# A four-layer float32 transformer on one core: the on-chip buffers get new start addresses

## The reference

```python
def first_block(x, ...):                       # two layers
    for l in range(DEPTH):
        n = rms_norm(h, attn_norm[l])
        h = h + (hybrid_mixer(n, ...) if l % 2 == 0 else diff_mixer(n, ...))
        h = h + conv_glu_ffn(rms_norm(h, ffn_norm[l]), ffn_w_up[l], ffn_conv_w[l], ffn_conv_b[l], ffn_w_down[l])
    return rms_norm(h, final_norm)

def conv_glu_ffn(n, w_up, conv_w, conv_b, w_down):      # D_FF = 2816
    gate, up = jnp.split(n @ w_up, 2, axis=-1)
    ...
    return (jax.nn.silu(conv) * up) @ w_down

def second_block(x, ...):                      # two layers
    h = layer_norm(x, ln_in_g, ln_in_b)
    for l in range(DEPTH):
        h = layer_norm(DN_ALPHA * h + token_mixers(h, ...), ln1_g[l], ln1_b[l])
        h = layer_norm(DN_ALPHA * h + conv_ffn(h, ...), ln2_g[l], ln2_b[l])
    return h
```

## Time and profile before

| | us |
|---|---|
| median of 3 runs | 2945.43 (2944.07 to 2948.2) |
| span of the profiled execution | 2941.9 |
| what lies around the span, against the median | 3.5 |
| busy: PE, PE weight loads | 2746.1, 2003.8 |
| busy: DVE, ACT, POOL | 1738.8, 1095.4, 1045.3 |

### The profile page before, as it was taken

How to read it: one execution, slowest core, us unless ns; L and a number is a source line. 1 busy time by engine, 2 the same in 40 slices (tenths; PEclk the granted TensorE clock), 3 DMA queues, 4 the chain that set the end, 5 groups by cost and what they waited for, 6 DMA issues and landing times.

```text
span 2941.9 us, 34757 instructions
## 1 busy us (share of the span) xinstructions
PE 2746.1 (93%) x11434; PEld 2003.8 (68%) x11434; DVE 1738.8 (59%) x2256; ACT 1095.4 (37%) x1682; POOL 1045.3 (36%) x385
## 2 busy tenths in 40 slices
PE   6999999999998999999698988999989998899997
PEld 5654788887764678888375455778757644577875
DVE  4645774576386576377559336827634944583672
ACT  2344322223144343222442545323345345532333
POOL 3210344443321244444144123544424411254442
PEclk9998999999998899999799999999999998999999
DMA  3210223232211123222111011222311110122231
GB/s 134 65 50 22 65 92 106 87 101 85 79 51 36 43 87 105 87 94 99 39 54 54 29 37 64 95 90 93 102 61 55 51 43 22 64 93 96 90 97 67
DMA packets 56070, 212.17 MB, mean 72 GB/s; under 512 B 6192, under 2 KB 6448, under 8 KB 55856
## 3 DMA queue, kind: packets, MB, share of 16 engines
q1 hardware_dynamic: 55120, 209.60, 21.5%
q10 hardware_dynamic: 864, 1.44, 0.2%
HBM read 208.92 MB, written 2.10 MB: 72 GB/s over the span
## 4 chain that ended last, share of the span: by engine, by line
PE 78%; DVE 9%; issue 5%; ACT 5%; POOL 2%; DVEq 1%; DMA 0%; ACTq 0%; POOLq 0%
PE bank_G L457 22%; PE bank_G L459 21%; PE bank_G L458 21%; PE bank_S L1086 4%; PE bank_O L1096 2%; PE bank_X L1106 2%; DVE mx L1978 2%; PE bank_S L504 1%; POOL wlo L404 1%; PE bank_X L1651 1%; DVE scores_t L1629 1%; POOL decayed L1771 1%; DVE probs L1159 1%; PE bank_O L1722 1%; PE bank_X L786 1%
## 5 line engine op out<-in xcount | busy, mean ns | idle before, releaser
L404 POOL TENSOR_TENSOR wlo<-raw,whi 128x1024 fp32r<-128x1024 f32 (+1 forms) x363 | 1002.3, 2762 | 1762.3 <-ACT whi L430 1762.2
L457 PE MATMUL bank_G<-n_hi,whi 128*128 128x512 f32 x2392 | 980.3, 410 | 62.3 <-DVE n_lo L561 29.7
L459 PE MATMUL bank_G<-n_hi,wlo 128*128 128x512 f32 x2392 | 948.9, 397 | 0.0
L458 PE MATMUL bank_G<-n_lo,whi 128*128 128x512 f32 x2392 | 947.8, 396 | 0.0
L457 PEld LDWEIGHTS bank_G<-n_hi,whi 128*128 128x128 f32 x2392 | 457.9, 191 | 208.7 <-issue 65.8
L430 ACT ACTIVATE whi<-raw 128x1024 fp32r<-128x1024 f32 (+1 forms) x363 | 403.5, 1111 | 371.7 <-PE bank_G L459 356.5
L459 PEld LDWEIGHTS bank_G<-n_hi,wlo 128*128 128x128 f32 x2392 | 456.6, 191 | 102.6
L458 PEld LDWEIGHTS bank_G<-n_lo,whi 128*128 128x128 f32 x2392 | 457.6, 191 | 98.7 <-issue 7.2
L627 DVE SCALAR_TENSOR_TENSOR h<-h,mixed 128x512 f32 (+1 forms) x96 | 70.1, 730 | 406.6 <-ACT mixed L436 406.6
L457 PE MATMUL bank_G<-a_hi,whi 128*128 128x512 f32 x704 | 279.1, 397 | 4.2 <-DVE a_lo L739 2.2
L459 PE MATMUL bank_G<-a_hi,wlo 128*128 128x512 f32 x704 | 279.4, 397 | 0.0
(11 more groups left out here) (280 smaller groups left out, 2606.5 us busy)
## 6 DMA issues: line engine op xcount, KB each, us to landing
raw<-in_w_mix_in SPq DMA_DIRECT2D x42, 512.0 KB, 3.3
raw<-in_w_out SPq DMA_DIRECT2D x32, 512.0 KB, 3.3
raw<-in_w_hyb_in SPq DMA_DIRECT2D x25, 512.0 KB, 3.3
raw<-in_w_diff_in SPq DMA_DIRECT2D x24, 512.0 KB, 3.3
raw<-in_w_up0a SPq DMA_DIRECT2D x22, 512.0 KB, 3.3
raw<-in_w_up0b SPq DMA_DIRECT2D x22, 512.0 KB, 3.3
raw<-in_w_up1a SPq DMA_DIRECT2D x22, 512.0 KB, 3.3
raw<-in_w_up1b SPq DMA_DIRECT2D x22, 512.0 KB, 3.3
```

Of the source, the lines that this page charges most:

```text
L404: pool.tensor_tensor(b.wlo[:, g.slot, 0:width], b.raw[:, g.slot, 0:width], b.whi[:, g.slot, 0:width], ALU.subtract).then_inc(b.lo_ready, 1)
L457: pe.matmul(out, b.whi[:, g.slot, w], hi[:, k, :], start=(k == 0), stop=False)
L458: pe.matmul(out, b.whi[:, g.slot, w], lo[:, k, :], start=False, stop=False)
L459: mm = pe.matmul(out, b.wlo[:, g.slot, w], hi[:, k, :], start=False, stop=(k == pieces - 1))
```

## The change

The order of allocation and the offsets change; the instruction streams of all five engines stay the same, instruction by instruction, except for the addresses.

- The small buffers (`vec`, `glmask`, `aup`, `small`, `table`, `lamp`, `den`, `rden`, `nmax`) come first; a padding buffer fills up to a multiple of 2048 bytes.
- All buffers made of rows follow from there, so each row starts at a multiple of 2048. `const` goes to the end.
- `posrow` no longer has its own space; it lies where `uq` lies. `posrow` is loaded at the start and read last in `rope2_dve` in the first layer; `uq` is first loaded in `mixer_act` in the third.
- In the arena the rows with padding (`gate`, `up`, `cpad`) go behind those without (`conv`, `conv_up`, `silu`, `prod`, `q_rope`).

```diff
+ROW = 4 * T
+ARENA = 21056
...
+    b.vec = sb("vec", [P, VEC.n])
+    b.glmask = sb("glmask", [P, GLA_LEVELS, P], U8)
+    b.aup = sb("aup", [P, P])
+    b.small = sb("small", [P, 16])
+    b.table = sb("table", [P, 1])
+    b.lamp = sb("lamp", [P, 4])
+    b.den = sb("den", [P, 6])
+    b.rden = sb("rden", [P, 6])
+    b.nmax = sb("nmax", [P, 6])
+    start = (nc.sbuf_base + 31) // 32 * 32
+    sb("pad", [P, -start % ROW // 4])
+
     b.h = sb("h", [P, KD, T])
     b.raw = sb("raw", [P, 2, W11])
     b.whi = sb("whi", [P, 2, W11], F32R)
     b.wlo = sb("wlo", [P, 2, W11], F32R)
-    b.const = sb("const", [P, CONST.n])
...
-    b.posrow = sb("posrow", [P, T], I32)
...
+    uq_at = nc.sbuf_base
+    b.uq = sb("uq", [P, 2, 3 * P])
+    b.posrow = nc.alloc_sbuf_tensor_at("posrow", [P, T], I32, offset=uq_at)
+    b.ukv = sb("ukv", [P, 4 * P])
     b.cos2 = sb("cos2", [P, T])
     b.sin2 = sb("sin2", [P, T])
...
-    low_at = (nc.sbuf_base + 31) // 32 * 32
-    sb("low", [P, 2 * KD * T + 8])
-    size = (nc.sbuf_bytes_remaining - 96) // 4
-    arena_at = (nc.sbuf_base + 31) // 32 * 32
+    low_at = nc.sbuf_base
+    sb("low", [P, 2 * KD * T])
+    arena_at = nc.sbuf_base
+    size = ARENA
     sb("arena", [P, size])
+    b.const = sb("const", [P, CONST.n])
+    for start in (low_at, arena_at):
+        assert start % ROW == 0, start
...
-    b.gate, n = at(arena_at, "gate", [P, T + 2 * PAD], F32, n)
-    b.up, n = at(arena_at, "up", [P, T + 2 * PAD], F32, n)
     b.conv, n = at(arena_at, "conv", [P, T], F32, n)
     b.conv_up, n = at(arena_at, "conv_up", [P, T], F32, n)
     b.silu, n = at(arena_at, "silu", [P, T], F32, n)
     b.prod, n = at(arena_at, "prod", [P, T], F32, n)
+    b.gate, n = at(arena_at, "gate", [P, T + 2 * PAD], F32, n)
+    b.up, n = at(arena_at, "up", [P, T + 2 * PAD], F32, n)
...
-    b.cpad, n = at(arena_at, "cpad", [P, 2, T + 2 * CPAD], F32, n)
-    b.q_rope, _ = at(arena_at, "q_rope", [P, T], F32, n)
+    b.q_rope, n = at(arena_at, "q_rope", [P, T], F32, n)
+    b.cpad, _ = at(arena_at, "cpad", [P, 2, T + 2 * CPAD], F32, n)
```

More of the change, by code:

```diff
@@ L196, in allocate @@
     b.wlo = sb("wlo", [P, 2, W11], F32R)
-    b.const = sb("const", [P, CONST.n])
-    b.vec = sb("vec", [P, VEC.n])
-    b.glmask = sb("glmask", [P, GLA_LEVELS, P], U8)
+    uq_at = nc.sbuf_base
+    b.uq = sb("uq", [P, 2, 3 * P])
+    b.posrow = nc.alloc_sbuf_tensor_at("posrow", [P, T], I32, offset=uq_at)
+    b.ukv = sb("ukv", [P, 4 * P])
     b.cos2 = sb("cos2", [P, T])
     b.sin2 = sb("sin2", [P, T])
-    b.uq = sb("uq", [P, 2, 3 * P])
-    b.ukv = sb("ukv", [P, 4 * P])
-    b.aup = sb("aup", [P, P])
-    b.posrow = sb("posrow", [P, T], I32)
-    b.small = sb("small", [P, 16])
-    b.table = sb("table", [P, 1])
-    b.lamp = sb("lamp", [P, 4])
     b.mixed = sb("mixed", [P, 2, T])
@@ L214, in allocate @@
     b.ntmp = sb("ntmp", [P, 2, T])
-    b.den = sb("den", [P, 6])
-    b.rden = sb("rden", [P, 6])
-    b.nmax = sb("nmax", [P, 6])
-    low_at = (nc.sbuf_base + 31) // 32 * 32
-    sb("low", [P, 2 * KD * T + 8])
-    size = (nc.sbuf_bytes_remaining - 96) // 4
-    arena_at = (nc.sbuf_base + 31) // 32 * 32
+    low_at = nc.sbuf_base
+    sb("low", [P, 2 * KD * T])
+    arena_at = nc.sbuf_base
+    size = ARENA
     sb("arena", [P, size])
+    b.const = sb("const", [P, CONST.n])
+    for start in (low_at, arena_at):
+        assert start % ROW == 0, start
     def at(region, name, shape, dtype=F32, offset=0):
         n = int(np.prod(shape[1:]))
-        limit = size - 8 if region == arena_at else 2 * KD * T
+        limit = size if region == arena_at else 2 * KD * T
         assert offset + n <= limit, (name, offset + n, limit)
```

## The result

The changed kernel takes **2928.8 us** (median of 9 runs, 2923.71 to 2940.73) against 2944.24 us for the kernel before on the same chip (9 runs, 2942.11 to 2955.77): ratio 0.9945, interval 0.9934 to 0.9956, 15.4 us between the medians. The profiled execution went from a span of 2941.9 to 2922.2 us, 19.7 us less (its own time is 2924.7 us). The forecast was 2936 us, 9.4 us less: the sign and the range from 2890 to 2978 held, the narrower range that the prediction gave its own case (2932 to 2943) did not. The gain was 1.6 times the forecast by the medians and twice it by the profiled spans, and it came from two products where one was expected.

A forecast was written before the change was run, and what follows sets the result against it. The prediction took TensorE's end-to-end matmuls to bound the kernel. The a products gave -9.4 us, n products, other engines and DMA nothing: 2945.4 - 9.4 = 2936 us, range 2890 to 2978.

The forecast's parts named there:

- its own case: Large products: a products reach the n products' rate, three matmuls in 685.5 to 689 ns; 2932 to 2943 us, chance 0.40.
- The bound: Whole launch: TensorE's matmuls run end to end, so any change per three matmuls counts 3096 times.
- The a products: Down stages: rows move from 32 to 0 modulo 64, three matmuls fall from 700 to 686.7 ns; 9.4 us gained.
- The n products: Up stages and other n matmuls: rows already start at a multiple of 64 bytes, so no change, between 91 us gain and 32 us loss.
- I take zero, between them: n matmuls: chose no change between a 91 us gain and a 32 us loss, since weight-slice crossings of 2048 cost nothing.
- 3096 x (t - 689.7): All n and a matmuls: total change in ns, with t the time of three matmuls after the change.
- I take that as the cause: Large matmuls: a rows starting 32 bytes behind a multiple of 64 explain 700 against 687 ns per three matmuls.
- The other engines and DMA: VectorE, ScalarE, GpSimd and loads: new start addresses change nothing that counts; costed at zero.
- Nothing happens: Large matmuls: the 700 against 687 ns has another cause than the 32 bytes; time stays at 2945 us, chance 0.16.
- Slower by collision: Large matmuls: equal starts make weight loads and moving rows meet; 700 ns per three, +32 us, 2977 us; slower: chance 0.22.
- Much faster: Large matmuls: whole excess goes, three fall towards 649 ns; 126 us gained, 2819 us; chance 0.13 for nearly the whole.
- What would show it: Stage signs: right if down0b's distance is 0.687 and up0b stays at 120.8 us; wrong if n matmuls change pace at all.

The follow-up runs named there:

- the map: Table from several kernels with weights, n rows or a rows moved: three matmuls take 680 to 703 ns by moving-row start minus weight-slice start, modulo 256 bytes.

## Why the prediction was right, and where it was not

**The bound** was read rightly in kind: what a triple gains is gained by the launch where TensorE runs end to end (the earlier trace rows and their counterparts above). "3096 times" was too many: the earlier trace rows are two stages of 24, and in the trace before 1909 of the 2392 n triples and 674 of the 704 a triples stand at their steady distance (684 to 690 and 698 to 702 ns from one L457 to the next).

**The a products (forecast -9.4 us).** The term was mis-sized. It took the n products' pace as the goal; the triple fell from 700 to 680, not to 687. 704 x 20 = 14.1 us by the steady distance; the 653 triples that are steady in both traces gave 13.1 us. Changed alone, these products gave 13.2 us of the profiled span and 9.4 us by the medians (6.5 to 13.0 by the interval).

**The n products (forecast 0).** The step that failed is "I take zero, between them". The triple fell by 6.7 ns, 2392 x 6.7 = 16 us at the steady distance. Set side by side triple by triple, the traces before and after show what became of it. 1664 triples went from some 687 to 680 ns and gave 11.1 us. 237 that had been steady became 1.0 us longer in all; 212 of them are among the first three behind a break. 8 became 3.2 us longer, six of these at a granted clock below 0.7. The other 483 were off their steady distance before already (breaks, waits, the lower clock) and became 0.3 us longer. That leaves 6.6 us; with 13.5 us of the a products and a first matmul that came 0.4 us later it is the 19.7 us of the span. Changed alone, the n products gave nothing that can be measured: `mix_in1`, with the split that meets L2012 and the lower clock, became 8.1 us longer and took all of it. So the formula 3096 x (t - 689.7) with t = 680 gives -30 us, of which two thirds came by the profiled spans and half by the medians: it holds neither the triples that do not run end to end, nor the first matmuls behind a break, nor the waits and the clock.

**Luck.** That the time lay in the range is in part luck. The one term of the sum had a wrong cause and came out a third too small, the other was put at nothing, and of the 16 us that it left out waits, breaks and the clock took more than half. By the same reasoning the kernel with the weights moved should have kept its n products at 687 ns, with their rows at multiples of 2048; they took 697, and that kernel 2965.23 us.

**The cause.** "I take that as the cause", of the 32 bytes of the moving row, was wrong, and one step ahead of it is where it went wrong: the weights were struck out because both products use the same slices. They are the same slices at a different distance. One pair of places could not tell a start from a distance; the earlier trace rows fit r = 64 and r = 96 as well as 0 and 32 modulo 64.

**The other engines and DMA (forecast 0)** held, row by row and with all other rows put at 32 modulo 64. What did not hold is that GpSimd and VectorE could be left out: their instructions last as long as before, but a faster TensorE shifts when they meet.

**The rivals.** *Nothing happens* is out. By the rule of the Trainium skill, "Advanced Engine Details and Errata", section "SBUF Cachelines", starts at multiples of 32 would all be as good as one another; the map, with 680 to 703 ns among eight such starts, differs from it as a whole account. *Slower by collision* had the mechanism in kind, two streams whose starts matter to each other, and the wrong sign: equal residues are the best place and not the worst. For the bad places its price was too high: a loss of 32 us was put down for triples of 700, and the kernels with n rows at 128 and 448 (triples of 697 to 700, one run each) took 28.4 and 22.6 us more than the kernel before on their chip, of which 16 and 8 us are the lower clock in the attention of `mix_in0` and `mix_in1`. The two independent read ports of "SBUF — State Buffer", section "Who interferes with whom", in the Trainium skill speak against any such dependence, and here the measurement decides: moving the weights alone, with the rows in place, changed the n triple from 680 to 697. *Much faster* fell with the crossing: rows that cross a multiple of 2048 run at 680 like those that do not. The 649 ns of its floor were not reached by any of the eight distances, and the 40 ns a triple above 640 (three times 512 columns at 2.4 GHz) stay open.

**What would show it.** The prediction said that it is wrong if the n triple moves at all, and it did; down0b's distance came out at 0.680, not 0.687, and up0b fell from 120.8 to 119.8. So by its own signs the prediction's account failed while its number held.

## What to carry to other kernels

Where matmuls run end to end at the upper clock, read the distance from one start to the next, not the duration of one; if it stands well above the columns divided by the clock (here 227 ns at best where 512 columns are 213), compare the start of the moving rows with that of the weight slices modulo 256, and give both the same residue before anything else in the layout is touched. One padding buffer did here what a new layout did. This is shown for fp32r matmuls of 512 columns with a new weight slice each, and for nothing else. Price such a gain by the stretches that run without a restart, and look for what a faster TensorE makes other engines meet: the n products, changed alone, gained nothing that could be measured.

## What the runs showed of the hardware that was not expected

- The pace of fp32r matmuls with weight loads between them depends on r as in the map: 680, 687, 697 to 703 ns for three matmuls of 512 columns. It repeats after 256 bytes (0 and 256 give 680, 64 and 320 give 687, 192 and 448 give 700) and does not depend on the absolute place. That two read streams meet is inferred from this and not shown; no view has them. The six matmuls at a granted clock of 0.50 took 427 ns each at r = 64, so there nothing is left of it.
- The pattern is not symmetric: 64 is good (687), 192 is not (700).
- After a restart it takes about three matmuls at r = 64 and five to eleven at r = 0 until the steady pace is there.
- A VectorE multiplication of some 740 ns that came up while a GpSimd split was running took 2823 ns and ended 0.55 us behind it (2315.30 against 2314.75); the one that was already running when a split began kept its time. So the maxima of some 2870 ns in the earlier trace rows need not be the taps' own.
- The granted clock differs between kernels whose instructions are the same. The kernel before shows a mean of 0.957 to 0.960 over its runs, the changed one 0.951 to 0.957, and its lowest clock goes with its slowest run (2940.73 us). The pace of the n products does not order this: the kernel with n rows at 128 (697 to 699 ns) shows 0.954, the one with n rows at 32 (700 ns) 0.963. Much of the difference lies in the attention at the end of `mix_in0` and `mix_in1`, which takes from 48.7 us at a clock of 0.89 to 58.5 us at 0.74. Why is not settled.
